# RMS factors applied behind the projections, a halved first slab and a regrouped conv opening in a two-block transformer kernel

## What is computed

```python
# first block
n = rms_norm(h, ln_mix_g)
qa, ka, va, qb, kb, vb, ga, gb = split(n @ w_in)
qa, ka = rope(qa), rope(ka)                 # x1*cos - x2*sin, x2*cos + x1*sin
ya = dilated_mixture(qa, ka, va) @ w_branch_a
yb = stick_breaking(qb, kb, vb) @ w_branch_b
h = h + (sigmoid(ga + b_a) * ya + sigmoid(gb + b_b) * yb) @ w_out
h = h + memory_cross_attn(rms_norm(h, ln_x_g), rms_norm(mem, ln_mem_g), ...)
n = rms_norm(h, ln_ffn_g)
u = causal_conv3(n @ w_up) + conv_b         # per channel, 3 taps
h = h + (silu(u_gate) * u_val) @ w_down
x = rms_norm(h, ln_f_g)                     # the input rows of the second block
# second block, twice: norm, w_in, three mixers, w_out, norm, feed-forward
p = rms_norm_2(x, norm1_g[l]) @ w_in[l]
a, u, v, cv, cg = split(p)
# pool mixer(a), gated mixer(u, v), 31-tap conv module(cv, cg); joined @ w_out
# l = 0: dense SwiGLU; l = 1: the two best of 8 experts
```

## Time and profile before

| quantity | value |
|---|---|
| median of 3 runs | 1937.9 us |
| lowest and highest of them | 1935.19 and 1938.63 us |
| profiled execution, its own time | 1936.7 us |
| its span | 1934.9 us |
| mean granted clock of PE | 0.985 |
| PE busy | 1857.2 us, 96% |
| DVE busy | 1481.6 us, 77% |
| ACT busy | 1169.7 us, 60% |

### The profile page before, as it was taken

How to read it: one execution, slowest core, us unless ns; L and a number is a source line. 1 busy time by engine, 2 the same in 40 slices (tenths; PEclk the granted TensorE clock), 3 DMA queues, 4 the chain that set the end, 5 groups by cost and what they waited for, 6 DMA issues and landing times. The chain is left out here.

```text
span 1934.9 us, 26118 instructions
## 1 busy us (share of the span) xinstructions
PE 1857.2 (96%) x10369; PEld 1613.8 (83%) x10369; DVE 1481.6 (77%) x1582; ACT 1169.7 (60%) x1103; POOL 56.0 (3%) x71
## 2 busy tenths in 40 slices
PE   6999998899999999997999999999999999999996
PEld 6988977899888999986888888888888888888884
DVE  6554576677786665696688989889898898988985
ACT  4446645555543444443677767677677777767773
POOL 0000000000320000320000000000000000000000
PEclk9999999999999999998899999999999999999998
DMA  8433433655451765454799999999999999999991
GB/s 299 147 110 125 144 124 109 223 198 196 119 187 61 239 196 196 116 190 164 263 351 369 362 346 370 346 357 364 343 374 353 354 367 334 375 358 349 368 363 40
DMA packets 258031, 495.71 MB, mean 256 GB/s; under 512 B 9609, under 2 KB 99439, under 8 KB 257903
## 3 DMA queue, kind: packets, MB, share of 16 engines
q1 hardware_dynamic: 253103, 488.65, 71.5%
q10 hardware_dynamic: 4800, 5.32, 0.9%
HBM read 492.89 MB, written 1.05 MB: 255 GB/s over the span
## 5 line engine op out<-in xcount | busy, mean ns | idle before, releaser
L376 DVE TENSOR_TENSOR splitL<-raw,splitH 128x2048 fp32r<-128x2048 f32 (+1 forms) x316 | 717.8, 2278 | 225.6 <-ACT splitH L372 214.4
L372 ACT ACTIVATE splitH<-raw 128x2048 fp32r<-128x2048 f32 (+1 forms) x316 | 598.1, 1901 | 162.8 <-PE bank L418 146.2
L416 PE MATMUL bank<-splitH,RBH 128*128 128x512 f32 x1184 | 471.0, 398 | 7.0 <-DVE splitL L376 6.0
L418 PE MATMUL bank<-splitH,RBL 128*128 128x512 f32 x1184 | 463.5, 391 | 0.0
L417 PE MATMUL bank<-splitL,RBH 128*128 128x512 f32 x1184 | 463.3, 391 | 0.0
L416 PE MATMUL bank<-RAH,splitH 128*128 128x256 f32 x1088 | 312.0, 287 | 4.9 <-DVE RAL L462 3.8
L417 PE MATMUL bank<-RAL,splitH 128*128 128x256 f32 x1088 | 308.1, 283 | 0.0
L418 PE MATMUL bank<-RAH,splitL 128*128 128x256 f32 x1088 | 308.0, 283 | 0.0
L376 DVE TENSOR_TENSOR splitL<-rawx,splitH 128x2048 fp32r<-128x2048 f32 x111 | 254.0, 2291 | 34.6 <-ACT splitH L372 32.2
L416 PEld LDWEIGHTS bank<-splitH,RBH 128*128 128x128 f32 x1184 | 223.7, 189 | 53.9 <-ACT fb L1375 5.8
L418 PEld LDWEIGHTS bank<-splitH,RBL 128*128 128x128 f32 x1184 | 223.3, 189 | 48.0
(11 more groups left out here) (296 smaller groups left out, 1866.4 us busy)
## 6 DMA issues: line engine op xcount, KB each, us to landing
raw<-in_moe_wd SPq DMA_DIRECT2D x75, 1024.0 KB, 6.7
raw<-in_moe_wg SPq DMA_DIRECT2D x57, 1024.0 KB, 6.4
raw<-in_moe_wu SPq DMA_DIRECT2D x56, 1024.0 KB, 7.0
rawx<-in_moe_wu SPq DMA_DIRECT2D x38, 1024.0 KB, 6.9
rawx<-in_moe_wg SPq DMA_DIRECT2D x37, 1024.0 KB, 6.9
rawx<-in_moe_wd SPq DMA_DIRECT2D x36, 1024.0 KB, 6.8
raw<-in_w_in SPq DMA_DIRECT2D x25, 1024.0 KB, 5.1
raw<-in_w_up SPq DMA_DIRECT2D x22, 1024.0 KB, 5.4
```

The lines of the kernel that those rows point to most:

```text
L372: a = act.op(lambda e: e.activation(h[:, 0:size], r[:, 0:size], ACT.Copy), self.landed[n], over)
L376: d = dve.op(lambda e: e.tensor_tensor(l[:, 0:size], r[:, 0:size], h[:, 0:size].bitcast(F), ALU.subtract), self.landed[n], over, a)
L416: e.matmul(o, lh, rh, start=start, stop=False)
L418: return e.matmul(o, ll, rh, start=False, stop=stop)
```

## The change

It has four parts, here named A, C, E and F as in the text further down.

**A, the opening.** `X` is turned and split unscaled as soon as it has landed. Slab 0 arrives as two DMAs and is split in two halves (`split_half`). The first two units run their first four chunks on the first half and then the other four on the second (`pair`). The row factor comes out of half sums and a root (`root_of`), is put on a diagonal (`diagonal`) and turned by PE into a tile `R1` that holds it along the columns (`over_columns`). `sinT` and `cosT` are multiplied by `R1` once, and so every rotated unit gets the factor. The value products get it as ACT's `scale` during evacuation; the query and key units of attention B and the keys of the memory are evacuated by DVE with `R1` or `R2` instead of by ACT. c1 is loaded on SP's queue behind slab 1. The squares of `M` stand at units 5 and 7, its transposes and splits in the value product "va".

**C, the gates.** The 16 evacuations move from ACT to DVE, where `SG` gets the factor `R1`. The bias goes into the sigmoids, and so these are 16 of 256 columns in place of 4 of 1024.

**E, the conv feed-forward's opening.** Step i = 0 is written out in `opening`: all four scalings, middle taps and DVE taps, with the two splits placed between them, in place of unit by unit.

**F, the first mixer.** `residual()` is called behind "mu" and no longer ahead of "mv", and the evacuation of "ma" waits for it.

```diff
@@ Weights
+                if n == 0:
+                    self.halves[0] = load(dst[:, 0:4, :], src[:, 0:4, :], eng=sp)
+                    parts = [(dst[:, 4:8, :], src[:, 4:8, :])]
...
+            def split_half(self, q):
+                r, (h, l), s = self.slots[self.where[0]][0], (splitH[0], splitL[0]), self.where[0]
+                o = slice(1024 * q, 1024 * q + 1024)
+                landed = self.halves[0] if q == 0 else self.landed[0]
+                a = act.op(lambda e: e.activation(h[:, o], r[:, o], ACT.Copy), landed)
+                d = dve.op(lambda e: e.tensor_tensor(l[:, o], r[:, o], h[:, o].bitcast(F), ALU.subtract), a, landed)
...
@@ opening of the first block
-        ts = norm_rows(X, scr, 0, lx, late=first_params)
-        nx, tn = norm_cols(scr, ts, "ln_mix_g", 0, nAH, nAL, tprm)
+        sq1[0, 0] = square_half(X, scr, 0, 0, 0, lx[0])
+        sq1[0, 1] = square_half(X, scr, 0, 0, 1)
+        sq1[1, 0] = square_half(X, scr, 0, 1, 0, lx[1])
...
+        nx = [split_rows(turned[k], "ln_mix_g", nAH, nAL, k) for k in range(4)]
+        turned.append(turn_rows(X, 7, lx))
+        W.split_half(0)
+        nx += [split_rows(turned[k], "ln_mix_g", nAH, nAL, k) for k in range(4, 8)]
+        W.split_half(1)
+        sq1[1, 1] = square_half(X, scr, 0, 1, 1, lx[1])
+        rx, trx = root_of(0, sq1)
+        tdx = diagonal(D1, rx, trx)
...
+        pair = [ps.take(), ps.take()]
+        for ks in (all8[:4], all8[4:]):
+            pair_t = [wstat(first, banks[pair[m]][:, 0:256], nAH, nAL, m, ks, ks[0][0] == 0, ks[0][0] == 4,
+                            ps.free[pair[m]], by=parts) for m in range(2)]
+        W.release(Wt[3], pair_t[1])
+        tRx = over_columns(R1, D1, tdx)
+        trig = [dve.op(lambda e, c=c: e.tensor_tensor(c, c, R1[:, :], ALU.mult), tRx, lc1) for c in (sinT, cosT)]
...
@@ gates
-                        sg_t[u, q] = act.op(lambda e, u=u, q=q, b=b: e.activation(
-                            SG[:, u, q, :], banks[b][:, 0:256], ACT.Identity, bias=pcol("b_gate", 8 * q + u)),
-                            t, attn_a.free)
+                        sg_t[u, q] = dve.op(lambda e, u=u, q=q, b=b: e.tensor_tensor(
+                            SG[:, u, q, :], banks[b][:, 0:256], R1[:, :], ALU.mult), t, attn_a.free)
...
@@ conv feed-forward, i == 0
+                scale(0)
+                rest = W.begin_split()
+                centre(0)
+                rest()
+                scale(1)
+                centre(1)
+                back(0)
+                tg = act.op(lambda e: e.activation(G[:, :, :], G[:, :, :], ACT.Silu), end[0, 0], end[0, 1])
+                rest = W.begin_split()
+                back(1)
...
@@ first mixer
-            if l == 0:
-                lz.rows.residual()
...
+            txg = lz.rows.residual() if l == 0 else None
...
-            row = put_r(lambda tb: at_rows[:, tb, :], ta)
+            row = put_r(lambda tb: at_rows[:, tb, :], ta, txg)
```

More of the change, by code:

```diff
@@ new lines, in diagonal, with over_columns, f @@
+        def diagonal(D, r, tr):
+            return [dve.op(lambda e, tb=tb: e.tensor_scalar(D[:, tb, :], ident, r[:, tb:tb + 1], None, ALU.mult),
+                           tr[tb]) for tb in range(2)]
+        def over_columns(R, D, td, *waits):
+            b = ps.take()
+            def f(e):
+                for tb in range(2):
+                    last = e.matmul(banks[b][:, 128 * tb:128 * tb + 128], ones, D[:, tb, :], start=True, stop=True)
+                return last
+            t = pe.op(f, td, lc, ps.free[b])
+            tR = act.op(lambda e: e.activation(R[:, :], banks[b][:, 0:256], ACT.Copy), t, *waits)
+            ps.free[b] = [tR]
+            return tR
@@ new lines, in turn_rows, with f, split_rows @@
+        def turn_rows(src, k, *waits):
+            b = ps.take()
+            def f(e):
+                for tb in range(2):
+                    last = e.transpose(banks[b][:, tb * 128:tb * 128 + 128], src[:, tb, k * 128:(k + 1) * 128], ident)
+                return last
+            return b, pe.op(f, ps.free[b], lc, *waits)
+        def split_rows(bt, gname, H, L, k):
+            b, t = bt
+            g = split_from_psum(H[:, k, :], L[:, k, :], banks[b][:, 0:256], t, tprm, scale=pcol(gname, k))
+            ps.free[b] = g
+            return g
@@ new lines, in program @@
+        R1 = at("R1", [128, 256], ph + 74 * KB + 512)
+        R2 = at("R2", [128, 256], ph + 72 * KB)
+        D1 = at("D1", [128, 2, 128], ph + 42 * KB)
+        sq1 = {}
+        sq1[0, 0] = square_half(X, scr, 0, 0, 0, lx[0])
+        sq1[0, 1] = square_half(X, scr, 0, 0, 1)
+        sq1[1, 0] = square_half(X, scr, 0, 1, 0, lx[1])
+        turned = [turn_rows(X, k, lx) for k in range(2)]
+        b = ps.take()
+        t = pe.op(lambda e, b=b: e.transpose(banks[b][:, 0:16], stage[0:16, 0, :], cb[0:16, 0:16]), loads, lc,
+                  ps.free[b])
@@ new lines, in program @@
+        tprm.append(act.op(lambda e, b=b: e.activation(prm[:, 0:16], banks[b][:, 0:16], ACT.Copy), t))
+        ps.free[b] = list(tprm)
+        turned += [turn_rows(X, k, lx) for k in range(2, 7)]
+        nx = [split_rows(turned[k], "ln_mix_g", nAH, nAL, k) for k in range(4)]
[4 more added lines that the diff above has]
+        sq1[1, 1] = square_half(X, scr, 0, 1, 1, lx[1])
@@ L666, in rope_finish @@
             qk_ready[unit] = t2
-        for unit in range(12):
[L669 to L674, removed]
+        Wt = W.take("qk", 1)
+        first = (Wt[0], Wt[1], None, Wt[3])
+        parts = {k: nx[k] + W.halves[k // 4] for k in range(8)}
+        pair = [ps.take(), ps.take()]
[5 more added lines that the diff above has]
+        trig = [dve.op(lambda e, c=c: e.tensor_tensor(c, c, R1[:, :], ALU.mult), tRx, lc1) for c in (sinT, cosT)]
+        sq2 = {}
+        for unit in range(12):
+            if unit < 2:
+                b, t = pair[unit], pair_t[unit]
+            else:
+                if unit % 2 == 0:
+                    Wt = W.take("qk")
+                b = ps.take()
+                t = wstat(Wt, banks[b][:, 0:256], nAH, nAL, unit % 2, all8, True, True, ps.free[b], by=nx)
+                if unit % 2:
+                    W.release(Wt[3], t)
             i = rope_n[0] % 2
             rope_n[0] += 1
-            wt = [t, lc1, tn, rfree[i]]
+            wt = [t, trig, rfree[i]]
             t1 = dve.op(lambda e, b=b, i=i: e.tensor_tensor(rsc[i], banks[b][:, 0:256], sinT, ALU.mult), *wt)
@@ L1337, in ffn @@
                             nn.extend(norm_cols(scr, ts, "ln_ffn_g", 0, nAH, nAL, ks=range(4, 8))[0])
-                            W.ahead(1)
+                            rest_of_split = opening(early, G, V, Y, ev)
                         else:
```

129 lines of the change are left out of this document (91 added, 38 removed).

## The result

The changed kernel took 1945.74 us (median of 6 runs, 1944.6 to 1949.29), the kernel before 1936.2 (6 runs, 1934.62 to 1938.63). The ratio is 1.005, with a 95% interval from 1.0037 to 1.0063: slower by some 9.5 us. The forecast was +3.1 us, inside what can't be told from no change, with 0.38 for slower. The time lies in the stated range, 1931 to 1947, but near its upper end, and the 9.5 are more than the 3.9 that the forecast called no measurable change. The profiled execution has a span of 1943.7 us at a mean granted clock of 0.981.

What follows compares the result with a forecast made beforehand. PE was taken as the bound, busy 1857.2 of 1934.9 us. Terms -6.5 (opening), +5.9 (gates), -7.4 (conv opening) and +11.1 (first mixer) gave +3.1, so 1941.0 us on the median's scale, range 1931 to 1947.

Steps and rivals of the forecast that it cites:

- The rotation product: Opening: the first rotation product was to begin at 21.4 us, where before it began at 26.37; -5.0 us.
- The term: Opening: earlier rotation product, a later wait removed and extra work for R2 sum to -6.5 us, bounds -4.5 and -7.6.
- the second wait: Gates: near 202 us PE waits 3.4 for a bank that DVE empties late, 2.4 more than before.
- slower* rival: Gates: PE's clock also falls behind the new waits, losing 1.9 us, for 1942.9; chance 0.38, including the gates' upper bound.
- DVE's backlog: First mixer: the moved root stands behind 17.74 us of gapless DVE work, making the band product 9.2 us late.
- The rival that the gates are free: Gates: evacuations on DVE find idle gaps, costing +1 us, for 1936.1 in all; chance 0.20.
- the stall-free mixer: First mixer: DVE reaches the root before PE reaches the band product, -6.0 us, for 1923.9 in all; chance 0.07.

Runs made afterwards that it cites:

- gates_pool: Changed kernel with the gates' banks emptied by ACT without bias and SG multiplied by R1 on POOL, 16 sigmoids kept; 1938.42 us.
- no_F: Changed kernel with residual() called ahead of the product mv again, as before the change; 1935.24 us.
- gates_act16: Changed kernel with the gates evacuated by ACT without bias, 16 sigmoids kept, the gates' R1 factor left out; 1938.05 us.
- pool_copies: Changed kernel with residual()'s root ahead of mv on DVE and its two copies of X on POOL straight behind it; 1929.59 us.
- best: Changed kernel with early root, X copies on POOL, and gates emptied by ACT then multiplied by R1 on POOL; 1927.20 us, ratio 0.9947.
- gates_act4: Changed kernel with the gates evacuated by ACT with bias and four sigmoids of 1024 columns, the gates' R1 factor left out; 1935.86 us.
- no_E: Changed kernel with the conv feed-forward's first step written unit by unit, as before the change; 1952.17 us.
- late_copies: Changed kernel with residual()'s root back ahead of mv on DVE, only ACT's two copies of X staying behind mu; 1933.95 us.
- A_alone: Changed kernel with the gates, conv-opening and first-mixer edits undone, leaving the opening and its evacuations; gates' R1 left out; 1930.47 us.
- before_E: Kernel before the change plus only the regrouped conv feed-forward opening; 1929.57 us, ratio 0.9964.
- before_F: Kernel before the change plus only the late residual() in the first mixer; 1949.53 us, ratio 1.0062.

## Why the forecast came out as it did

**A.** The rotation product came at 21.32 for 21.4, in part by luck: the pair began 0.3 later than forecast, and its slow phase ended after 12 matmuls and not after 24. The term was 1.0 too large in this trace. The missing step is the clock behind the wait of 1.80 for the first rotated unit: the shift goes from -5.05 to -3.49 there, a loss of 1.6. Nine of the ten traces with this opening show it, with the first two rotation products 4.9 apart; in gates_pool's they are 3.41 apart and the clock stays at 1.00. Where the slow phase of the pair ends differs between executions too. At one and the same matmul (76.30 in the kernel before) the shift was -5.4 to -5.9 in five of the traces that hold the new opening (the changed kernel, no_F, gates_act16, pool_copies, best), -6.7 to -7.2 in four (gates_act4, no_E, late_copies, A_alone), and -8.5 in gates_pool. The Trainium skill, "TensorE: Matmul & The Clock Gate", Part 1 (The HAM clock gate), says that the slow phase's end varies from run to run. The traces agree that it varies: 12 slow matmuls in the changed kernel's and none in gates_act4's. The range of A, -4.5 to -7.6, held all but one.

**C.** The direction was right, the size was short by 2.9. Up to the second wait the sum held: forecast +4.0, and the shift goes from -5.17 ahead of the gates to -1.20 at 198.68. Its terms came otherwise than written, though. PE reached the suffix sums 2.3 late for a forecast 2.4, but through two waits, one of 0.82 at 169 that I had not counted and one of 1.17; DVE's split stood 0.6 back and not 0.4, and PE began as the first evacuation was through and not the second, and these two errors largely cancel. The second wait was 3.15 for 3.4 (the numbers written there, 202.6 less the 198.92 at which PE was free, give 3.7 before what the chain is late).

Three things were missing. The clock fell behind the 3.15, the mechanism of the *slower* rival, and took 1.5. It fell in each of the five traces that have this wait (0.80, 0.78, 0.84, 0.83 and 0.72 over 200 to 206), and stayed 1.00 in the others, where ACT empties the banks. The sigmoids, priced by a copy of the same shape at 0.37, took 0.41 each, 2.6 in place of 1.9, and with the mix behind them the shift grows by 3.0; undone by themselves they give back 2.2 by medians. And 0.3 went in attention A, ahead of the gates. So the step that failed is that the forecast sum leaves the clock alone behind a wait of 3.4; next to it, the sigmoids and the mix were priced 1.1 too low.

**E.** Right in place and size: -7.5, wait 0.50 for 0.5, clock 1.00. before_E shows it alone, and no_E shows the same wait coming back. What the forecast missed is that E also costs something later: all nine traces with E have a wait for `RBL` of 0.7 to 1.2 near 500 and lose 0.9 to 1.5 with it, and the four without E (the kernel before, before_F, no_E, A_alone) have no such wait. The wait for `X` behind it is 2.4 to 2.5 with E and 2.1 without. How the regrouping at the first step leads to a wait at the last one, no run shows.

**F.** The mechanism was right in each step, down to the 17.74 us of DVE's backlog and the 15.54 of PE's wait for a forecast 15.9. The size was 10.0 for 11.1 in the profiled execution (10.3 with the next few matmuls), by medians 10.5 (no_F) and 12.5 (before_F). What was missed is that the slow stretch behind it has no fixed length: 1.9 was forecast for it, and 1.3 to 4.5 were lost.

**The rest.** I let nothing change behind the four parts. The 1.1 between 348 and 511 is the later cost of E just named. The 1.4 at the end is the net of small gains and of 1.7 at the last expert's product, and chance is its likely reading, since it goes with none of the parts: all 13 traces have the same wait of 2.02 or 2.03 there, and behind it the clock over 5 us is 0.66 to 0.68 in six (the changed kernel, no_F, no_E, gates_act16, late_copies, best) and 1.00 in seven, the kernel before among them.

The sum was -6.5 + 5.9 - 7.4 + 11.1 = +3.1, and it came out as -5.5 + 8.8 - 7.5 + 10.0 + 2.5 = +8.3 between the profiled executions, with 8.8 between their spans and 9.5 between the medians. The rival that the gates are free fell with gates_act4, the stall-free mixer with the trace of the changed kernel. Of the rival *slower*, the mechanism was the true one, but the clock in the gates, 1.5, is less than a third of the miss of 5.2 between the profiled executions; the clock behind the first rotated unit (1.6) and at the last expert's product (1.7) made as much each, and F, 1.1 under its forecast, hid part of it.

## What to carry to other kernels

Where work moves behind other work on an in-order engine, add up what stands ahead of it there without a gap; that sum gave the stall to within half a microsecond, whereas the moved work itself was 4 us. Moving an evacuation to another engine can cost by the bank it holds and not by its own time; it can be cured by emptying the bank where it was emptied and doing the arithmetic afterwards on an idle engine. Four changes put together can hide a good one: E alone was worth 0.36%, and together with the others it was lost. And work on POOL isn't free for DVE: a tap beside POOL's copies took 0.57 to 0.58 us in place of 0.41.

## What the runs showed that I had not expected

PE came back at 1.2 GHz after waits of 3.15 us in the gates, in five traces of five, and after 1.80 to 1.91 us behind two small products early in the program, in nine of ten. After one and the same wait of 2.03 us near the end it did so in six traces of 13, and in the kernel before it was at full clock after 2.08. So a wait of about 2 us gave no sure clock in these traces. A stall of 15.5 us was followed by 1.3 to 1.7 us of loss in four traces and by 4.3 to 4.5 in two. And POOL, at 0.9 us for 128 columns with a new scalar each, took only 4.9 for 1024 columns, but DVE's taps beside it took 2.9 for five in place of 2.06.
